# Start addresses of the down products' weights and activation rows, relative to one another in 256 bytes

## What is computed

```
def swiglu_ffn(x, w_gu, w_down):
    gu = x @ w_gu                                  # 1024 -> 2 x 2816
    gate, up = jnp.split(gu, 2, axis=-1)
    return (jax.nn.silu(gate) * up) @ w_down       # 2816 -> 1024, the "down products"
...
    e = p @ ple_w_proj[l]                          # 256 -> 1024, in the same buffers
```

## Time and profile before

| | us |
|---|---|
| median of 3 executions | 2091.97 |
| lowest and highest | 2088.49, 2093.28 |
| the profiled execution, device time | 2089.16 |
| its span in the profile | 2087.0 |
| TensorE busy in it | 2047.6 (98%) |
| VectorE, ScalarE, GpSimd busy | 1183.3, 678.8, 71.6 |
| granted TensorE clock, mean | 0.998 |

### The profile page before, as it was taken

One profiled execution on the slowest core, in us unless ns is written; L12 is line 12 of the kernel. 1 busy time (PEld: TensorE's weight loads), 2 busy tenths in 40 slices (PEclk: granted clock), 3 DMA queues, 4 the chain that ended last, 5 costly groups with the idle time before them and its releaser, 6 DMA issues. The chain is left out here.

```text
span 2087.0 us, 34476 instructions
## 1 busy us (share of the span) xinstructions
PE 2047.6 (98%) x13041; PEld 2032.3 (97%) x13041; DVE 1183.3 (57%) x2367; ACT 678.8 (33%) x1401; POOL 71.6 (3%) x110
## 2 busy tenths in 40 slices
PE   7999999999999999999999999999999999999998
PEld 7999999999999999999999999999999999999997
DVE  5643554354534579547876855345544554368776
ACT  5321222122212234317774532212121212124555
POOL 0000000000000001330000000000000000000000
PEclk9999999999999999999999999999999999999999
DMA  5180111011101101322121211011101111021112
GB/s 168 61 116 26 60 60 43 17 60 60 50 16 55 60 1 51 72 63 45 41 83 61 81 62 61 10 50 60 60 19 41 60 60 38 22 81 42 62 41 104
DMA packets 153277, 116.17 MB, mean 56 GB/s; under 512 B 72648, under 2 KB 143628, under 8 KB 153200
## 3 DMA queue, kind: packets, MB, share of 16 engines
q1 hardware_dynamic: 117728, 108.41, 16.7%
q10 hardware_dynamic: 33424, 5.67, 2.0%
q0 software_dynamic: 2048, 1.06, 0.3%
HBM read 105.96 MB, written 9.15 MB: 55 GB/s over the span
## 5 line engine op out<-in xcount | busy, mean ns | idle before, releaser
L852 PE MATMUL ps<-x_hi,w_lo 128*128 128x352 f32 x2688 | 884.1, 329 | 9.4 <-DVE w_lo L2118 5.1
L854 PE MATMUL ps<-x_hi,w_hi 128*128 128x352 f32 x2688 | 863.7, 321 | 0.0
L853 PE MATMUL ps<-x_lo,w_hi 128*128 128x352 f32 x2688 | 863.7, 321 | 0.0
L852 PEld LDWEIGHTS ps<-x_hi,w_lo 128*128 128x128 f32 x2688 | 506.5, 188 | 12.5 <-issue 6.6
L853 PEld LDWEIGHTS ps<-x_lo,w_hi 128*128 128x128 f32 x2688 | 507.4, 189 | 0.0
L854 PEld LDWEIGHTS ps<-x_hi,w_hi 128*128 128x128 f32 x2688 | 505.2, 188 | 0.0
L852 PE MATMUL ps<-a_hi,wd_lo 128*128 128x352 f32 x1104 | 357.9, 324 | 3.7 <-DVE acc L2916 2.9
L854 PE MATMUL ps<-a_hi,wd_hi 128*128 128x352 f32 x1104 | 354.8, 321 | 0.0
L853 PE MATMUL ps<-a_lo,wd_hi 128*128 128x352 f32 x1104 | 354.6, 321 | 0.0
L2277 DVE TENSOR_TENSOR acc<-ps,acc 128x352 f32<-128x352 f32 x480 | 250.3, 523 | 83.8 <-PE ps L854 77.7
L2212 DVE TENSOR_TENSOR tmp_u<-ps,rstd_pre 128x352 f32<-128x352 f32 x132 | 68.9, 523 | 337.2 <-PE ps L854 337.2
(11 more groups left out here) (226 smaller groups left out, 1564.6 us busy)
## 6 DMA issues: line engine op xcount, KB each, us to landing
raw<-in_ffn_w_gu_dram SPq DMA_DIRECT2D x88, 512.0 KB, 3.5
rawd<-in_ffn_w_down_dram SPq DMA_DIRECT2D x22, 1024.0 KB, 7.6
raw<-in_w_in_dram SPq DMA_DIRECT2D x16, 512.0 KB, 4.3
raw<-in_w_out_dram SPq DMA_DIRECT2D x16, 512.0 KB, 3.8
raw<-in_ple_w_gate_dram SPq DMA_DIRECT2D x16, 512.0 KB, 3.7
toeplitz<-rev ACTq DMA_DIRECT2D x8, 512.0 KB, 8.3
x_in<-in_x_prompt_dram SPq DMA_DIRECT2D x4, 512.0 KB, 9.6
toep_first<-toeplitz SPq DMA_DIRECT2D x32, 64.0 KB, 2.3
```

The lines of the kernel that those rows point to most:

```text
L852: eng.matmul(dst, wl, xh, start=first, stop=False)
L853: eng.matmul(dst, wh, xl, start=False, stop=False)
L854: return eng.matmul(dst, wh, xh, start=False, stop=last)
```

## The change

Four things are done, all of them to places in memory. The down weights are placed so that `wd_lo` begins at 0 and `wd_hi` at 128. `a_hi` and `a_lo` become twelve tensors, one for each chunk, hidden tile and part; those of chunk 0 begin at 0, of chunk 1 at 128, of chunk 2 at 64, for both hidden tiles and both parts. To make room, `ones` shrinks from 128 columns to the two that are read, and `tmp_a` becomes another name of `tmp_u`, so that the product is written over its own operand. `tmp_u` may then be written anew only when `a_lo` has been made from it, so the wait of `scaled` for the up tile is on `a_lo_done` in place of `prod_done`, with the same count. `rawd` moves ahead of the `tmp` buffers, and `y_stage` overlaps `rawd` first in place of `tmp_g`. All other operands of the wide, mixer and output products keep their places in 256 bytes.

```diff
+LINE = 64
+A_LINES = ((0, 0), (2, 2), (1, 1))
+WD_LINES = (0, 2)
...
+        def tile_at_line(name, shape, line, dt=F32R):
+
+            at[0] += (4 * LINE + line * LINE - at[0]) % (4 * LINE)
+            return place(name, shape, dt)
...
-        ones = tile("ones", [P, P])
+        ones = tile("ones", [P, 2])
...
-        a_hi = tile("a_hi", [P, G, TOK], F32R)
-        a_lo = tile("a_lo", [P, G, TOK], F32R)
-        wd_hi, wd_at, _ = place("wd_hi", [P, G * D], F32R)
-        wd_lo = tile("wd_lo", [P, G * D], F32R)
+        act = {(c, t, part): tile_at_line(f"a_{part}{c}{t}", [P, C], A_LINES[c][part == "lo"])[0]
+               for c in range(NC) for part in ("hi", "lo") for t in range(G)}
+        wd_hi, wd_at, _ = tile_at_line("wd_hi", [P, G * D], WD_LINES[1])
+        wd_lo = tile_at_line("wd_lo", [P, G * D], WD_LINES[0])[0]
+        rawd, rawd_at, _ = place("rawd", [P, G * D])
         tmp_g, tmp_at, _ = place("tmp_g", [P, 2, C])
         tmp_u = tile("tmp_u", [P, 2, C])
         tmp_s = tile("tmp_s", [P, 2, C])
-        tmp_a = tile("tmp_a", [P, 2, C])
-        rawd, rawd_at, _ = place("rawd", [P, G * D])
+        tmp_a = tmp_u
...
-                        mm = passes(dst, wd_hi[:, sl], wd_lo[:, sl], a_hi[:, t, cols(c)],
-                                    a_lo[:, t, cols(c)], t == 0, t == G - 1)
+                        mm = passes(dst, wd_hi[:, sl], wd_lo[:, sl], a_hi(c, t),
+                                    a_lo(c, t), t == 0, t == G - 1)
...
-                    eng.wait_ge(prod_done if up else silu_done, q - 1)
+                    eng.wait_ge(a_lo_done if up else silu_done, q - 1)
```

More of the change, by code:

```diff
@@ L341, in build @@
         st_rows = place("st_rows", [P, NJ * P], offset=wd_at + 4 * 3 * P)[0]
-        p_in = place("p_in", [P, 3 * NC, PLE], offset=tmp_at)[0]
-        y_stage, _, e = place("y_stage", [P, 9, D // 2], offset=tmp_at)
-        assert e <= ffn_end
+        p_in, _, e = place("p_in", [P, 3 * NC, PLE], offset=tmp_at)
+        assert e <= nc.sbuf_usable_end
+        y_stage, _, e = place("y_stage", [P, 9, D // 2], offset=rawd_at)
+        assert e <= nc.sbuf_usable_end
         tenth = (WIDE0["ple"] + PLE_SEQ[10][1]) % 2
@@ L401, in f32, with a_hi, a_lo @@
             return t.bitcast(F32)
+        def a_hi(c, t):
+            return act[c, t, "hi"][:, :]
+        def a_lo(c, t):
+            return act[c, t, "lo"][:, :]
         def lru_a(p):
@@ L951, in half @@
                     mm = passes(ps[:, off % BANKS, 0:C], wd_hi[:, sl], wd_lo[:, sl],
-                                a_hi[:, t, cols(c)], a_lo[:, t, cols(c)], t == 0, t == G - 1)
+                                a_hi(c, t), a_lo(c, t), t == 0, t == G - 1)
                     if t == G - 1:
@@ L1330, in ple_proj @@
                         sl = slice(k * D + (2 * q + t) * P, k * D + (2 * q + t) * P + P)
-                        mm = passes(dst, wd_hi[:, sl], wd_lo[:, sl], a_hi[:, k, cols(c)],
-                                    a_lo[:, k, cols(c)], k == 0, k == PT - 1)
+                        mm = passes(dst, wd_hi[:, sl], wd_lo[:, sl], a_hi(c, k),
+                                    a_lo(c, k), k == 0, k == PT - 1)
                     mm.then_inc(psum_full, 1)
@@ L1517, in hidden_hi @@
                     eng.wait_ge(psum_full, STEP * i + (R - STEP + 4 * NC + KT * (c + 1)))
-                eng.activation(a_hi[:, h, cols(c)], tmp_a[:, h, :], ACT.Copy).then_inc(a_hi_done, 1)
+                eng.activation(a_hi(c, h), tmp_a[:, h, :], ACT.Copy).then_inc(a_hi_done, 1)
             def hidden_chunk(f, i, c, next_half, hook=None):
@@ L1665, in p_features @@
                     eng.wait_ge(psum_full, n + 1)
-                    eng.activation(a_hi[:, k, cols(c)], ps[:, n % BANKS, 0:C], ACT.Copy
+                    eng.activation(a_hi(c, k), ps[:, n % BANKS, 0:C], ACT.Copy
                                    ).then_inc(pt_hi, 1)
@@ L2228, in hidden_lo @@
                 eng.wait_ge(a_hi_done, q + 1)
-                eng.tensor_tensor(a_lo[:, h, cols(c)], tmp_a[:, h, :], f32(a_hi[:, h, cols(c)]),
+                eng.tensor_tensor(a_lo(c, h), tmp_a[:, h, :], f32(a_hi(c, h)),
                                   ALU.subtract).then_inc(a_lo_done, 1)
@@ L2384, in p_features @@
                     eng.wait_ge(pt_hi, PT * c + k + 1)
-                    eng.tensor_tensor(a_lo[:, k, cols(c)], ps[:, n % BANKS, 0:C],
-                                      f32(a_hi[:, k, cols(c)]), ALU.subtract
+                    eng.tensor_tensor(a_lo(c, k), ps[:, n % BANKS, 0:C],
+                                      f32(a_hi(c, k)), ALU.subtract
                                       ).then_inc(psum_free, 1)
```

## The result

The change makes the kernel slower. Its median is 2105.82 us (7 runs, 2104.17 to 2117.25) against 2091.97 us for the kernel before (7 runs, 2088.49 to 2101.99). The ratio is 1.0068, with a 95% interval from 1.0047 to 1.0089. The forecast was 2091.5, and its range ended at 2102.

The account below looks back on a forecast made before the run. TensorE's own pace was taken to bound the kernel. Down products at +0.6 us and all else at 0 gave 2089.8 on the profiled execution and 2092.6 on the median; a value between, 2091.5, was forecast, range 2079 to 2102.

Parts of the forecast that it names:

- What bounds the kernel: Whole kernel: TensorE, busy 98% of the span at full clock, so only its own time counts.
- Wait, alias, buffers: 0: The wait on `a_lo_done`, the product written over its operand and the moved buffers: each priced at 0.
- The down products, mixed from the constant cases: +0.6 us: Down passes: mean of three chunks 159.15 ns against 158.96 now, +0.2 ns x 3312 = +0.6 us.
- the constant cases: Trace stretches with fixed relations: rows and weights at the same place, 160.0 ns; rows 128 bytes off, 157.9 ns.
- the 7.58 to 7.74 us that I allowed: Down chunk 2 in a loop step: time outside this range would show the prediction wrong; each chunk took 7.63 us.
- The gate products: Gate passes behind chunk 2: addresses unchanged, another starting phase, priced at nothing; 6.8 us at 160.0 ns, 14.4 at 161.2.
- the sign of being wrong: Gate block in a loop step, 45.77 us: a move by more than 0.1 us would show the prediction wrong.
- the slower rival: Down chunk 2 ends in a phase from which gates go on at 160.0 ns: +10 us, 2102; chance 0.23.
- every loop step is back at 158.9 in both kinds of products: Loop steps, down and gate passes: 158.9 ns although distances change order at each chunk; argued against a slow lock spreading.
- The two ports: TensorE reads moving rows and weights over independent SBUF ports, so addresses have no share and the change gives 0 us.
- The steps of 6.67 ns: Passes until addresses repeat take whole steps of 6.67 ns (16 columns), so the pace locks into a few values.
- The faster lock: Rival: down addresses repeat after three passes; 157.8 ns throughout gives -3.8 us, 155.6 gives -11 us; chance 0.33.

Follow-up runs that it names:

- The first kernel of bare passes: No layer, TensorE alone: 284 streams of 36 passes with rows and weights at chosen multiples of 64 bytes, entered after 256 to 270 columns; 157.75 to 166.7 ns per pass.
- the two kernels in which it takes 26.50 us: Kernel after with wide weights moved; down products with relations of before (first, 2097.47 us) or rows at 0, both weights at 128 (second, 2118.53 us).

## Why the prediction was wrong, point by point

**What bounds the kernel.** Right. TensorE's pace was all that moved, and 14.3 us of paces stand against 13.9 us of time.

**Wait, alias, buffers: 0.** Right; the kernel with the old relations shows all three together at ratio 1.0007, with the same loop step.

**The down products, mixed from the constant cases: +0.6 us.** This term was mis-sized: it measured +4.1 us. Chunk 1 was forecast at 159.3 and took 159.32. Chunk 2 was forecast at 159.55 and took 160.64, within the 7.58 to 7.74 us that I allowed (7.71). Chunk 0 was forecast at 158.6, as the fastest, and was the slowest, 160.96. The step that failed is "I mix the constant cases", with "I take the mix, since the loop's own pace is just such a mix". That equality (158.96 against 158.95) was a coincidence: the same alternation locks at 158.9, 160.0 or 161.1, and the bare relation of chunk 0 makes 161.1 though two of its three passes lie 128 bytes from their load. A pace belongs to a whole period of passes, not to each pass. Chunk 1's agreement was luck: it settles at 158.9, and its 159.32 is a mean with the first six passes at 160.7.

**The gate products: "I cost this at nothing in the sum".** This is the step that failed by most: priced at 0, it measured 10.2 us with the other wide products, almost all of the 10.5 us that the range had above the forecast. A gate block moved by 0.55 us, where 0.1 was the sign of being wrong. The mechanism was written down as the slower rival, and the runs bear it out: the addresses of the gates are untouched, matmuls of 64 to 76 columns ahead of them settle them at 158.9, 160.0 or 161.1 ns, and chunk 2's rows at 128 bring them back to 45.77 us. It was priced at 160.0 for all three chunks, and they took 161.2, 161.2 and 160.1; with the 4.1 us of the down products that makes 14 instead of 10, and the 3.8 us by which the median is over the range. The block count was off the other way: I multiplied by 22 blocks, and 17 of the 18 whole gate blocks in the loops show the new paces.

**The argument against it, "every loop step is back at 158.9 in both kinds of products".** It failed for a simple reason: 17 of the 18 gate blocks of the loops before are entered from the same alternation, so they show one entry, many times over, and say nothing on what another entry does. The last step of the second feed-forward showed a slow lock go over from down to gate products. It should have weighed more than 22 repetitions of one case.

**The two ports.** By the Trainium skill (page "TensorE: Matmul & The Clock Gate", section "Step-by-step: what each phase is for") loading weights takes nothing from the running matmul, and I read that as no share for the addresses. The first kernel of bare passes has 157.75 to 166.7 ns for the same instructions at other places, so for these fp32r passes with a load each, the addresses do have a share. With rows and low weights both at 0, moving the high weights alone by 64 bytes changes the pace from 161.1 (seven of eight entries) to 160.0 ns (all eight). No run has passes without a load, so whether a load takes something from the running matmul or is slow by itself isn't parted. The 149.2 ns that the prediction sets beside the loop's 158.96 comes from what that page gives, in its section "Back-to-back issue gap", for an isolated matmul and not for a stream with a load ahead of each, so it was no test of the ports.

**The steps of 6.67 ns.** Right in kind: 158.9, 160.0 and 161.1 are 143, 144 and 145 of them in six passes. But three passes don't take whole steps in every relation; 158.3 is 95/4 of one per pass. The faster lock at 155.6 was in no stream; the shortest seen, with different lines for low and high rows, was 157.75, from two to four of eight entries.

**What stays open.** That relation and entry together set the pace is shown; what in the memory or in TensorE's queue makes the lock is not, nor why a slow gate phase needs both halves of the change. No run predicts from addresses alone which pace an entry gives. Each kernel has one profiled execution; within it the settled paces repeat from loop step to loop step.

## What to carry to other kernels

Where passes run back to back with a weight load each, measure the pace of each block from starts in the timeline, and look at the blocks *behind* the one that is edited: here 10.2 of 14.3 us fell on products that nobody touched. A pace that repeats in every loop step is one sample of an entry, so when an edit shifts the end of a block, price the next block at the other paces that the trace shows, with a fair chance. And where something stands ahead of a block, such as an added matmul, take the pace from the settled passes; the first ones carry a cost of their own. Placements that a bare stream shows as fast can be had (here 0.1%), but the fastest ones here also had slow entries, and only the whole kernel says which one it takes.

## What the runs showed that I had not expected

- The spread: the same pass of 352 columns takes 157.75 to 166.7 ns by the places of its operands in 256 bytes and by the phase of entry. The slow twin of the fastest relation that the kernel used (158.3) is the slowest (166.7), 8.4 ns x 3312 = 28 us if the down products fall into it.
- An added matmul can make a kernel faster: one of 64 or 72 columns per step took the gate block of the kernel after from 46.32 to 45.98 and 45.88 us, its own 0.11 us included.
- Relations don't survive a shift in a simple way: bare streams with rows 128 bytes from both weights, all entered after 256 columns, took 158.3 ns with the weights at 0 and 192, and 166.7 with the weights at 64 and 128.
- The stretch of 27 us at 1.2 GHz in the mixer comes and goes between executions of one kernel and costs about 11 us, with TensorE as busy ahead of it (29.43 of 30 us) as where it doesn't come (29.35 in the kernel with the old relations). A wait of TensorE for ScalarE's `lru_r` stands just ahead of it in the kernel after, 1.84 us long, and the same wait is 1.84 us in the kernel before, without the stretch.
- ScalarE's issuing of the `toeplitz` DMAs ends between 127 and 135 us of the span; in the two kernels in which it takes 26.50 us (it ends at 132.3 and 134.6) it costs TensorE 3.0 us of waiting, and in the first of them a slower clock behind it.
